# A fourth pair of PSUM banks for the small steps between input and output projection

## The chip, the cores and the metric

The kernel runs on one core of a Trainium2 chip. The metric is the device time of one execution in microseconds (us). A core has a matrix engine (TensorE, in profiles PE), a vector engine (VectorE, DVE), a scalar engine (ScalarE, ACT), a general engine (GpSimd, POOL) and a queue engine that only issues transfers here (SyncE, SP). TensorE writes its results to PSUM, which has eight banks of 128 partitions x 512 float32 values; VectorE and ScalarE read them out. The engines run their own instruction lists in order and meet at semaphores.

## The reference, cut to what matters

One inference step of a two-layer encoder, for a prompt of 256 rows (two tiles of 128, called tile 0 and 1) and a sample of 32 rows (tile 2), all float32:

```
for l in range(2):
    z = rms_norm(x, ln_attn[l]) @ w_in[l]                # input projection, 1024 -> 1184
    # group A: 8 heads, 2 kv heads, QK-norm, rotary, window of 128 rows, learned sinks
    # group B: q from a 256-wide latent (b_w_uq), k and v from a 128-wide latent (b_w_ukv),
    #          norm of every head, shared rotary key, chunk-causal mask, 8 heads
    o = concat(softmax(q_a k_a) v_a, softmax(q_b k_b) v_b)
    x = x + o @ w_o[l]                                   # output projection
    h = rms_norm(x, ln_ffn[l])
    x = x + (swiglu(h) if l == 0 else top2_of_8_experts(h))
```

The new keys, values and latents of both layers are outputs too.

## The kernel before

Each engine's attention work is written out by hand as a list of steps for each layer: `PE_ORDER`, `ACT_ORDER`, `DVE_ORDER`. A step has a kind and a tile, an item or a group:

- `h t`: transpose the normalised rows of tile t (L1645). `za t c q`: input projection of tile t, column half c, reduction half q (L1726); `za 2` (L1696) and `zc t` (L1739) are the rest of it. ScalarE reads `za` out of PSUM by squares and a copy (L908, L909).
- `tq t`: transposes of queries, keys and latents of tile t (L1761 to L1765), after VectorE has normalised and rotated them (`z2`, last instruction L1231).
- `item i`: projection from a latent to keys and values (L1789) or to queries (L1781). VectorE normalises it straight out of PSUM (`i2`: L1375 for keys, L1367 and L1368 for queries, then more steps to L1231), and only then is its PSUM free. `titem i`: its transposes (L1801), copied out by ScalarE (L977).
- `s g`: scores of group g (L1822, L1826, L1836). VectorE adds the mask and takes the maximum (L1400, L1402); ScalarE takes exponentials (L994). For tile 2 the scores stay in PSUM until ScalarE has read them.
- `p g`: transposes of the probabilities (L1851, L1855, L1856), copied out by ScalarE (L1009, L1013). `o g`: probabilities times values (L1883, L1891). `to t`: transposes of the head outputs. `wo t c q` and `wo 2`: output projection (L1726, L1713). `hf t`, `ro t`: what the second half of the layer needs.

`za` and `wo` of tiles 0 and 1 accumulate in bank 0 (column half 0) or bank 1 (column half 1). All other steps are "small" steps and take a pair of banks, a room. There are three rooms, banks 2-3, 4-5 and 6-7, taken in turn over both layers:

```
return small_full, small_out, n % 3, n // 3 + 1, 2 + 2 * (n % 3), 2
```

`wait_room` lets TensorE write a room only after its last tenant was read out (`emptied[i] >= n - 1`); `full` and `free` count fills and releases. So a small step waits until the small step three places earlier in `PE_ORDER` has been read out.

The order of layer 0's small steps around the change: ..., p 0, titem 1, o 0, tq 0, zc 1, titem 2, item 3, s 1, item 4, p 1, tq 1, o 1, titem 3, titem 4, to 2, item 5, wo 2, item 6, s 2, titem 5, s 3, titem 6, hf 2, p 2, s 4, o 2, p 3, ..., s 6, to 0, p 5, s 7, and then the first `wo` of tile 0. In layer 1: ..., titem 2, (last `za` of tile 1), item 4, titem 3, s 1, s 2, o 0, titem 4, p 1, s 3, zc 1, o 1, p 2, to 2, p 3, o 2, o 3, wo 2, tq 1, to 0, ...

After the attention, layer 0 has the dense SwiGLU (L1943, L1959) and layer 1 eight experts in turn (L2027, L2047), whose weights ScalarE and VectorE split into a high and a low part. SP loads all weights through a ring of six slots; a slot is loaded again when the steps that read it are over.

Of the kernel before, what the change touches and what calls it, by code (L numbers as in the profile page):

```python
# [44 lines left out]
DEPTH = 2  # L45
# [105 lines left out]
def in_small(step):  # L151

    return step[0] in OPENS or step in (("za", 2), ("wo", 2))
# [57 lines left out]
    return ev  # L211


def ffn_jobs():

    jobs = [(m, i) for i in range(DCH) for m in ("gate", "up")]
    for c in range(2):
        jobs += [("dn", c, h) for h in range(2)]
        jobs += [("tz", d) for d in range(4 * c, 4 * c + 4)]
    return jobs + [None, ("pos",)]  # L220


def build(nc, a, out, consts):
# [3 lines left out]
    fills = [0] * RING  # L227
# [7 lines left out]
    for n, key in enumerate(plan):  # L235
        prev = [k for k in plan[n % RING:n:RING] if k is not None]
        if key is not None and prev:
# [4 lines left out]
    MOE_EVENTS = moe_events()  # L242
    per_expert = len(EXPERT) // RING
    assert len(EXPERT) % RING == 0
    SMALL = [(s_[0], l, *s_[1:]) for l in range(DEPTH) for s_ in PE_ORDER[l] if in_small(s_)]
    BANKED = [[(s_[0], l, s_[1], c) for l in range(DEPTH) for s_ in PE_ORDER[l] if s_[0] in IN_BANK and s_[2:] == (c, 0)]
              for c in range(2)]
    FFN_JOBS = ffn_jobs()
    place = {key: ("small", n) for n, key in enumerate(SMALL)}
    place.update({key: ("bank", n) for b in BANKED for n, key in enumerate(b)})  # L250
    place.update({key: ("ffn", n) for n, key in enumerate(FFN_JOBS)})
    SQUARES, ROOTS_X, ROWS_X = nth(ACT_ORDER, "zev", "zcev"), nth(ACT_ORDER, "n1", "n2"), nth(DVE_ORDER, "x1", "x2")
# [5 lines left out]
    with ExitStack() as ctx:  # L258
# [3 lines left out]
        def sem(name):  # L262
            return ctx.enter_context(nc.semaphore(name))
# [152 lines left out]
        loaded_cache = sem("loaded_cache")  # L416
        ukv_ready = sem("ukv_ready")
        w_ready = [sem(f"w_ready{i}") for i in range(RING)]
        small_full = [sem(f"small_full{i}") for i in range(3)]
        small_out = [sem(f"small_out{i}") for i in range(3)]  # L420
        bank_full = [sem(f"bank_full{i}") for i in range(2)]
        bank_out = [sem(f"bank_out{i}") for i in range(2)]
        ffn_full = [sem(f"ffn_full{i}") for i in range(4)]
# [85 lines left out]
        def found(key):  # L509

            family, n = place[key]
            if family == "small":
                return small_full, small_out, n % 3, n // 3 + 1, 2 + 2 * (n % 3), 2
            if family == "bank":
                return bank_full, bank_out, key[3], n + 1, key[3], 1
            return ffn_full, ffn_out, n % 4, n // 4 + 1, 2 * (n % 4), 2

        def pair(key, rows=P):

            *_, b, n = found(key)  # L520
            return ps[0:rows, b:b + n, :].rearrange("p a b -> p (a b)")
# [10 lines left out]
        def wait_full(eng, key):  # L532
            filled, _, i, n, *_ = found(key)
            eng.wait_ge(filled[i], n)

        def wait_out(eng, key):
            _, emptied, i, n, *_ = found(key)
            eng.wait_ge(emptied[i], n)

        def wait_room(eng, key):  # L540
            _, emptied, i, n, *_ = found(key)
            if n > 1:
                eng.wait_ge(emptied[i], n - 1)

        def full(ins, key):
            filled, _, i, *_ = found(key)
            ins.then_inc(filled[i], 1)
# [1075 lines left out]
        def _(pe):  # L1623
# [16 lines left out]
            def turn(key, src, rows):  # L1640

                wait_room(pe, key)
                v = pair(key)
                for k in range(KD):
                    ins = tr(v[:, k * P:k * P + rows], src[0:rows, k * P:(k + 1) * P], ident[0:rows, 0:rows])  # L1645
                full(ins, key)

            def turn_back(key, src_T, src):

                wait_room(pe, key)  # L1650
                wait_out(pe, src)
                v = pair(key)
                for t in range(3):
                    ins = tr(v[0:ROWS[t], t * P:(t + 1) * P], src_T[:, TOFF[t]:TOFF[t] + ROWS[t]], ident)
                full(ins, key)

            for l in range(DEPTH):
                for step in PE_ORDER[l]:
                    kind, *which = step
                    if kind == "hf" and l == 1:  # L1660

                        t, = which
                        key, r = ("hf", l, t), ROWS[t]
                        wait_room(pe, key)
                        if t == 1:
                            wait_out(pe, ("wo", l, t, 0))
# [524 lines left out]
```

## Time and profile before

| | us |
|---|---|
| median of 3 runs | 1339.23 (1337.82 to 1339.36) |
| the profiled execution | 1339.84 |
| its span, first to last instruction | 1338.0 |
| attention of layer 0 | about 15 to 176 |
| attention of layer 1 | about 398 to 557 |
| experts | about 557 to 1338 |

The mean granted clock of TensorE over the span is 0.972 of full speed; the granted clock of a stretch (PEclk) is 1.00 at 2.4 GHz and 0.50 at 1.2 GHz. In a row of the timeline the number after the start is the time that the merged instructions took, and the bracket behind it is the idle time of the engine before them, with the instruction that ended it. Rows of transposes show as PE MATMUL with `cst` (the identity) on one side. Times within the span are counted from its start.

### The profile page before, as it was taken

The numbers are of one execution on the slowest core, as the hardware profiler recorded it, in microseconds if no ns is written. First come the engines' busy times: TensorE is split into PE (matmuls) and PEld (weight loads), VectorE is DVE, ScalarE is ACT, GpSimd is POOL, SyncE is SP. The second block draws the span as 40 slices with busy tenths as digits, with TensorE's granted clock in tenths as the row PEclk, the third lists the DMA queues.
The fourth block names the chain that finished last, engine by engine and source line by source line (L and its number), as shares of the span: only waits on it lengthen the run. The fifth ranks groups of instructions, "written<-read, shape, count | busy, mean of one in ns | idle before, by whom it ended". The sixth has DMA issues, their size and how long they took to land.

```text
span 1338.0 us, 18390 instructions
## 1 busy us (share of the span) xinstructions
PE 1285.5 (96%) x6905; PEld 1050.8 (79%) x6905; DVE 938.1 (70%) x917; ACT 795.7 (59%) x793; POOL 146.2 (11%) x130
## 2 busy tenths in 40 slices
PE   5978989999989999999999999999999999999998
PEld 3457579999985467588888888888888888888886
DVE  1647344454334656468898898898898888888987
ACT  2446433433323456256787787777877867867774
POOL 2011000000000010010040040120130300300500
PEclk9978989999999989889999999999999999999999
DMA  8251085544250341669999999999999999999994
GB/s 303 55 122 33 0 253 166 178 158 143 79 185 0 74 125 57 221 237 335 371 383 378 367 396 374 369 397 366 362 411 355 376 397 352 393 387 373 373 405 163
DMA packets 124673, 350.35 MB, mean 262 GB/s; under 512 B 8768, under 2 KB 34080, under 8 KB 124624
## 3 DMA queue, kind: packets, MB, share of 16 engines
q1 hardware_dynamic: 120192, 336.05, 69.0%
q0 software_dynamic: 4032, 12.43, 3.1%
q10 hardware_dynamic: 400, 1.20, 0.2%
q8 instruction: 33, 0.54, 0.2%
q14 instruction: 16, 0.13, 0.0%
HBM read 340.70 MB, written 8.95 MB: 261 GB/s over the span
## 4 chain that ended last, share of the span: by engine, by line
PE 93%; DVE 3%; ACT 2%; issue 1%; DMA 1%; SPq 0%; DVEq 0%; ACTq 0%
PE ps L2027 36%; PE ps L2047 17%; PE ps L1943 11%; PE ps L1726 8%; PE ps L1959 5%; PE ps L1836 1%; PE ps L2035 1%; PE ps L1883 1%; PE ps L1789 1%; PE ps L2001 1%; PE ps L1781 1%; PE ps L1801 1%; PE ps L1645 1%; PE ps L1713 1%; PE ps L1891 1%
## 5 line engine op out<-in xcount | busy, mean ns | idle before, releaser
L1169 DVE TENSOR_TENSOR w_lo<-ring,w_hi 128x2048 fp32r<-128x2048 f32 (+1 forms) x322 | 675.6, 2125 | 180.3 <-ACT w_hi L845 176.8
L845 ACT ACTIVATE w_hi<-ring 128x2048 fp32r<-128x2048 f32 (+1 forms) x322 | 567.3, 1782 | 220.3 <-PE ps L2047 66.4
L2027 PE MATMUL ps<-w_hi,xg_hi 128*128 128x512 f32 (+1 forms) x768 | 288.9, 376 | 0.4 <-DVE xg_lo L1556 0.4
L2027 PE MATMUL ps<-w_hi,xg_lo 128*128 128x512 f32 (+1 forms) x768 | 287.1, 374 | 0.0
L2027 PE MATMUL ps<-w_lo,xg_hi 128*128 128x512 f32 (+1 forms) x768 | 286.2, 373 | 0.0
L2027 PEld LDWEIGHTS ps<-w_hi,xg_hi 128*128 128x128 f32 x768 | 145.2, 189 | 26.3 <-issue 0.5
L2027 PEld LDWEIGHTS ps<-w_lo,xg_hi 128*128 128x128 f32 x768 | 144.9, 189 | 26.0
L2027 PEld LDWEIGHTS ps<-w_hi,xg_lo 128*128 128x128 f32 x768 | 145.2, 189 | 25.2
L2047 PE MATMUL ps<-w_hi,am_hi 128*128 128x512 f32 x340 | 133.8, 393 | 0.0
L2047 PE MATMUL ps<-w_lo,am_hi 128*128 128x512 f32 x340 | 132.5, 390 | 0.0
L2047 PE MATMUL ps<-w_hi,am_lo 128*128 128x512 f32 x340 | 132.4, 389 | 0.0
L1726 PE MATMUL ps<-ring,hT 128*128 128x512 f32 x256 | 114.4, 596 | 0.0
L1943 PE MATMUL ps<-hT_hi,w_hi 128*128 128x288 f32 x352 | 105.3, 299 | 4.1 <-DVE hT_lo L1461 4.1
L789 POOL TENSOR_TENSOR tick<-cst 128x1 f32<-128x1 f32 x22 | 44.9, 2040 | 573.0 <-ACT y_out L1119 473.1
L1943 PE MATMUL ps<-hT_lo,w_hi 128*128 128x288 f32 x352 | 104.8, 298 | 0.0
L1943 PE MATMUL ps<-hT_hi,w_lo 128*128 128x288 f32 x352 | 104.4, 297 | 0.0
L1726 PEld LDWEIGHTS ps<-ring,hT 128*128 128x128 f32 x256 | 47.3, 191 | 52.4 <-issue 52.2
L2047 PEld LDWEIGHTS ps<-w_lo,am_hi 128*128 128x128 f32 x340 | 63.8, 188 | 13.5
L2047 PEld LDWEIGHTS ps<-w_hi,am_lo 128*128 128x128 f32 x340 | 63.9, 188 | 12.9
L2047 PEld LDWEIGHTS ps<-w_hi,am_hi 128*128 128x128 f32 x340 | 63.9, 188 | 12.8
L1943 PEld LDWEIGHTS ps<-hT_hi,w_hi 128*128 128x128 f32 x352 | 66.9, 190 | 4.5 <-issue 4.5
L1943 PEld LDWEIGHTS ps<-hT_hi,w_lo 128*128 128x128 f32 x352 | 67.3, 191 | 0.0
(308 smaller groups left out, 1446.3 us busy)
## 6 DMA issues: line engine op xcount, KB each, us to landing
ring<-in_moe_w_down SPq DMA_DIRECT2D x80, 1024.0 KB, 8.1
ring<-in_moe_w_gate SPq DMA_DIRECT2D x64, 1024.0 KB, 7.2
ring<-in_moe_w_up SPq DMA_DIRECT2D x64, 1024.0 KB, 9.2
ring<-in_moe_w_gate SPq DMA_DIRECT2D x32, 768.0 KB, 7.3
ring<-in_moe_w_up SPq DMA_DIRECT2D x32, 768.0 KB, 6.1
ring<-in_ffn_w_gate SPq DMA_DIRECT2D x11, 1024.0 KB, 5.4
ring<-in_ffn_w_up SPq DMA_DIRECT2D x11, 1024.0 KB, 5.3
ring<-in_ffn_w_down SPq DMA_DIRECT2D x10, 1024.0 KB, 5.1
```

The costliest lines, as they stand in the source:

```text
L789: pool.tensor_tensor(tick[:, i:i + 1], C("ident")[:, 0:1], C("ident")[:, 0:1], ALU.mult)
L845: A(hi[:, 0:size], src[:, 0:size], ACT.Copy).then_inc(hi_ready, 1)
L1169: V.tensor_tensor(lo[:, 0:size], src[:, 0:size], hi[:, 0:size].bitcast(F32), ALU.subtract).then_inc(lo_ready, 1)
L1645: ins = tr(v[:, k * P:k * P + rows], src[0:rows, k * P:(k + 1) * P], ident[0:rows, 0:rows])
L1713: ins = mm_(pair(key)[DEC * j:DEC * j + DEC, 0:256], hT[:, k, TOFF[2]:TOK], slot(wk, 4, 512)[:, k % 4, 256 * (j % 2):256 * (j % 2) + 256], ...
L1726: ins = mm_(pair(key), hT[:, k, TOFF[t]:TOFF[t] + P], slot(wk, 4, 512)[:, k % 4, :], start=(k == 0), stop=(k == KD - 1))
L1781: ins = mm_(pair(key, r)[:, c0:c0 + w], cqT[:, k, TOFF[t]:TOFF[t] + r], slot(("uq", l), 2, 768)[:, k, c0:c0 + w], start=(k == 0), stop=(k ...
L1789: ins = mm_(pair(key, r)[:, c0:c0 + 512], ckvT[:, KOFF[t]:KOFF[t] + r], w_ukv[:, c0:c0 + 512], start=True, stop=True)
L1943: ins = mm_(pair(key)[:, 512 * f:512 * f + TOK], w[:, k, f * P:(f + 1) * P], x[:, k, :], start=(k == 0 and m == 0), stop=(k == KD - 1 and ...
L1959: ins = mm_(pair(("dn", i, d // 2))[:, 512 * (d % 2):512 * (d % 2) + TOK], w[:, k, d * P:(d + 1) * P], x[:, kk, :], start=(kk == 0 and m = ...
L2027: ins = mm_(ps[:, b + c0 // 512, 0:c1 - c0], (xg_hi, xg_lo)[xp][:, k, :], w[wp][:, k % 2, c0:c1], start=(k == 0 and n == 0), stop=(k == KD ...
L2047: ins = mm_(ps[:, 6 + half, :], (am_hi, am_lo)[xp][:, c % 2, k0 + k, :], w[wp][:, k, 512 * half:512 * half + 512], start=(first and k == 0 ...
```

## The change

Between the last `za` of tile 1 and the first `wo` of tile 0, banks 0 and 1 hold nothing. The change makes them a fourth room (number 3) for the small steps of that stretch. `rooms()` gives every small step its room and its number among the fills of the room: inside the stretch the rooms go round by four, outside it by three. The stretch is given by two steps of `PE_ORDER` of each layer, both left out of it: from `za 1 1 1` to `s 7` in layer 0, from `za 1 0 1` to `to 0` in layer 1. Room 3 is taken eight times in layer 0 (tq 0, s 1, o 1, item 5, titem 5, p 2, s 5, s 6) and four times in layer 1 (s 1, p 1, p 2, o 3). The first tenant of room 3 in a layer (tq 0 in layer 0, s 1 in layer 1) also waits until both banks of `za 1` have been read out, and each of the two `wo` of tile 0 waits until all tenants of room 3 have been.

```diff
--- before.py
+++ after.py
@@ -211,6 +211,29 @@
     return ev
 
 
+SPARE_ROOM = [(("za", 1, 1, 1), ("s", 7)), (("za", 1, 0, 1), ("to", 0))]
+
+
+def rooms():
+
+    small, place, fills, last = [], {}, [0] * 4, -1
+    opens, closes = {}, []
+    for l in range(DEPTH):
+        first, end = (PE_ORDER[l].index(step) for step in SPARE_ROOM[l])
+        for i, step in enumerate(PE_ORDER[l]):
+            if not in_small(step):
+                continue
+            last = (last + 1) % (4 if first < i < end else 3)
+            fills[last] += 1
+            key = (step[0], l, *step[1:])
+            small.append(key)
+            place[key] = ("small", (last, fills[last]))
+            if last == 3 and l not in opens:
+                opens[l] = key
+        closes.append(fills[3])
+    return small, place, opens, closes
+
+
 def ffn_jobs():
 
     jobs = [(m, i) for i in range(DCH) for m in ("gate", "up")]
@@ -242,11 +265,10 @@
     MOE_EVENTS = moe_events()
     per_expert = len(EXPERT) // RING
     assert len(EXPERT) % RING == 0
-    SMALL = [(s_[0], l, *s_[1:]) for l in range(DEPTH) for s_ in PE_ORDER[l] if in_small(s_)]
+    SMALL, place, opens_spare, spare_fills = rooms()
     BANKED = [[(s_[0], l, s_[1], c) for l in range(DEPTH) for s_ in PE_ORDER[l] if s_[0] in IN_BANK and s_[2:] == (c, 0)]
               for c in range(2)]
     FFN_JOBS = ffn_jobs()
-    place = {key: ("small", n) for n, key in enumerate(SMALL)}
     place.update({key: ("bank", n) for b in BANKED for n, key in enumerate(b)})
     place.update({key: ("ffn", n) for n, key in enumerate(FFN_JOBS)})
     SQUARES, ROOTS_X, ROWS_X = nth(ACT_ORDER, "zev", "zcev"), nth(ACT_ORDER, "n1", "n2"), nth(DVE_ORDER, "x1", "x2")
@@ -416,8 +438,8 @@
         loaded_cache = sem("loaded_cache")
         ukv_ready = sem("ukv_ready")
         w_ready = [sem(f"w_ready{i}") for i in range(RING)]
-        small_full = [sem(f"small_full{i}") for i in range(3)]
-        small_out = [sem(f"small_out{i}") for i in range(3)]
+        small_full = [sem(f"small_full{i}") for i in range(4)]
+        small_out = [sem(f"small_out{i}") for i in range(4)]
         bank_full = [sem(f"bank_full{i}") for i in range(2)]
         bank_out = [sem(f"bank_out{i}") for i in range(2)]
         ffn_full = [sem(f"ffn_full{i}") for i in range(4)]
@@ -510,7 +532,8 @@
 
             family, n = place[key]
             if family == "small":
-                return small_full, small_out, n % 3, n // 3 + 1, 2 + 2 * (n % 3), 2
+                room, fill = n
+                return small_full, small_out, room, fill, (2 + 2 * room) % 8, 2
             if family == "bank":
                 return bank_full, bank_out, key[3], n + 1, key[3], 1
             return ffn_full, ffn_out, n % 4, n // 4 + 1, 2 * (n % 4), 2
@@ -541,6 +564,11 @@
             _, emptied, i, n, *_ = found(key)
             if n > 1:
                 eng.wait_ge(emptied[i], n - 1)
+            if key in opens_spare.values():
+                for c in range(2):
+                    wait_out(eng, ("za", key[1], 1, c))
+            if key[0] == "wo" and key[2] == 0:
+                eng.wait_ge(small_out[3], spare_fills[key[1]])
 
         def full(ins, key):
             filled, _, i, *_ = found(key)
```

## Rows read from the trace of the kernel before

**Rows 1.** Section 1 of the page: busy time, share of the span and instructions of each engine.

```profile
PE 1285.5 (96%) x6905; PEld 1050.8 (79%) x6905; DVE 938.1 (70%) x917; ACT 795.7 (59%) x793; POOL 146.2 (11%) x130
```

**Rows 2.** Windows, all engines: busy us (x instructions), then PEclk, DMA share, GB/s.

```profile
500.00:1338.00 838.00, 828.71 (x3989) 687.02 (x3987) 700.14 (x477) 594.21 (x424) 119.00 (x62) 0.99 0.91 344
```

**Rows 3.** Waits of PE over the span: us in total, times, longest.

```profile
PE ps L1836 <- DVE rt L1368: 7.0, 2, 4.4
```

**Rows 4.** Timeline, PE, layer 0: start us, us, instructions [idle before <-releaser].

```profile
67.05 0.66 PE L1761 MATMUL ps<-cst,qa 128*128 128x128 f32 x4
...
73.33 2.85 PE L1781 MATMUL ps<-ring,cqT 128*128 128x512 f32 x8
81.03 0.45 PE L1855 MATMUL ps<-cst,sp__65 128*128 128x128 f32 x1 [4.85 <-DVE tmp L1375]
...
81.92 1.06 PE L1761 MATMUL ps<-cst,qa 128*128 128x128 f32 x4
...
86.76 5.64 PE L1891 MATMUL ps<-vb,pT 128*32 128x64 f32 x32 [2.93 <-DVE rt L1368]
92.32 3.52 PE L1801 MATMUL ps<-cst,qkb 128*96 128x128 f32 x16
...
101.30 2.85 PE L1781 MATMUL ps<-ring,cqT 128*128 128x512 f32 x8
...
110.66 3.76 PE L1836 MATMUL ps<-kTb,qTb 96*128 96x128 f32 x16 [4.41 <-DVE rt L1368]
114.21 1.92 PE L1801 MATMUL ps<-cst,qkb 128*96 128x128 f32 x8
...
121.95 1.09 PE L1851 MATMUL ps<-cst,sp__65 128*128 128x128 f32 x8 [0.34 <-ACT sp__65 L994]
...
134.77 3.60 PE L1726 MATMUL ps<-ring,hT 128*128 128x512 f32 x8
```

**Rows 5.** Timeline, DVE (VectorE), layer 0.

```profile
79.86 0.19 DVE L1231 TENSOR_TENSOR kr<-rt,rt 128x32 f32<-128x32 f32 x1
...
112.02 0.42 DVE L1231 TENSOR_TENSOR qkb<-tmp 128x256 f32<-128x256 f32 x1
...
131.50 1.23 DVE L1400 TENSOR_TENSOR sp__65<-ps,cst 128x1024 f32<-128x1024 f32 x1 [1.29 <-PE ps L1836]
```

**Rows 6.** Timeline, ACT (ScalarE), layer 0.

```profile
65.71 0.59 ACT L909 ACTIVATE z<-ps 128x512 f32<-128x512 f32 x1
...
76.02 0.20 ACT L994 ACTIVATION_READ_ACCUMULATOR sp__65<-ps,nb 128x1 f32 x1
...
82.16 0.38 ACT L1013 ACTIVATE pT<-ps 128x256 f32<-128x256 f32 x1 [3.57 <-PE ps L1856]
```

**Rows 7.** Windows of 4 us, layer 0, same columns as rows 2.

```profile
76.00:80.00 4.00, 0.18 (x1) 0.00 (x0) 3.86 (x15) 2.56 (x6) 0.00 (x0) 0.81 1.08 225
...
92.00:96.00 4.00, 4.00 (x22) 3.67 (x22) 0.29 (x1) 1.08 (x2) 0.00 (x0) 0.55 0.00 0
...
108.00:112.00 4.00, 1.34 (x6) 1.37 (x7) 3.84 (x11) 3.53 (x15) 0.00 (x0) 0.65 0.24 82
```

**Rows 8.** Timeline, PE, layer 1.

```profile
458.83 0.75 PE L1826 MATMUL ps<-kTb,qTb 96*32 96x160 f32 x16
462.15 1.16 PE L1836 MATMUL ps<-kTa,qTa 64*128 64x128 f32 x16 [2.57 <-DVE rt L1368]
...
468.09 2.02 PE L1836 MATMUL ps<-kTb,qTb 96*128 96x128 f32 x16 [0.32 <-ACT qTb L977]
...
483.39 5.96 PE L1713 MATMUL ps<-ring,hT 128*32 128x256 f32 x64
```

**Rows 9.** Timeline, ACT, layer 1.

```profile
455.98 0.59 ACT L909 ACTIVATE z<-ps 128x512 f32<-128x512 f32 x1
```

**Rows 10.** Windows, layer 1, same columns as rows 2.

```profile
464.00:468.00 4.00, 3.78 (x17) 2.94 (x16) 3.23 (x8) 1.02 (x2) 0.00 (x0) 0.57 1.07 222
...
479.00:480.00 1.00, 1.00 (x12) 1.00 (x10) 0.97 (x2) 0.78 (x2) 0.00 (x0) 1.00 0.26 102
```

## The prediction

> **What bounds the kernel now.** I read four views in this order. The page and the stretches come first: TensorE is busy 96% of the span, and from 500 us on 828.71 of 838 us at an upper-level clock, while VectorE and ScalarE are filled less [rows 1, 2]. Whatever is won ahead of 500 us therefore reaches the end unless something other than TensorE starts an expert; the expert phase has no term in the sum. The waits of TensorE come second. In the two attention stages the ones to notice are releases by VectorE of PSUM that the next step does not read: L1368 and L1375 read an `item` out of PSUM, but the waiting instructions are L1836 (`s`), L1855 (`p`) and L1891 (`o`), which have nothing to do with an item [rows 3, 4]. They wait for a room. Third, the timeline gives the lengths: 4.85, 2.93 and 4.41 us in layer 0, 2.57 us in layer 1, together 14.8 us [rows 4, 8]. Fourth, the windows give the clock. In layer 0 the level fell to 1.2 GHz at about 78.5 us (mean 0.81 over 76 to 80), some 2.3 us after TensorE ran empty, and rose at about 95.6 us (0.55 over 92 to 96); it fell again at about 109.2 us (0.65 over 108 to 112) [rows 7]. So the waits also make later matmuls slow.
>
> **Why no room wait can get longer.** TensorE works in order. Before, step i needs the room of step i-3; inside the stretch it now needs that of i-4, which step i-1 had to have before. The first few steps of the stretch keep their i-3, and the first tenant of room 3 finds it empty. Everything else of a step's conditions is as it was, and outside the stretch the distance is again 3. So the rotation alone only removes constraints. What is added is two waits where room 3 is opened and one ahead of each of the two `wo` steps of tile 0; they are a few semaphore instructions, costed at nothing if satisfied.
>
> - Opening, layer 0: `tq 0` started at 67.05; the last bank of `za 1` was read by 66.30 (65.71 + 0.59) [rows 4, 6]. Cover 0.75 us, and neither end moves, since nothing ahead of them changes.
> - Opening, layer 1: `s 1` at 458.83 against 456.57 [rows 8, 9]. Cover 2.3 us. If either cover were gone, `tq 0` or `s 1` and all behind it would start later by what is missing.
> - Closing, layer 0: the last tenant of room 3 is `s 6`, read by 132.73; the first `wo` of tile 0 started at 134.77 [rows 4, 5]. Cover 2.0 us, and three other steps of TensorE lie between `s 6` and `wo` whatever moves. Layer 1 closes with `o 3`, long before its `wo`.
> - No DMA, no VectorE and no ScalarE instruction is added or moved. SP's queue waits for the same steps' ends.
>
> **Part A, layer 0, around items 3 and 4.** `item 4` ends at 76.18 (73.33 + 2.85). `p 1` waited for item 3's room; now it has another and needs only the exponentials, ready at 76.22. It starts at 76.4 instead of 81.03 and takes 0.5 us. But what is behind it, `tq 1`, needs VectorE's rows, which end at 80.05 (79.86 + 0.19) [rows 4 to 6]. So most of the first wait turns into a wait for data: `tq 1` starts at 80.1 instead of 81.92, 1.8 us earlier. `o 1` waited for item 4's room until 86.76; now it needs the copy of `p 1`, for which ScalarE had stood idle 3.57 us [rows 6], so it follows `tq 1` directly. TensorE still has 3.2 us without work after `p 1`, so I take the clock to fall as before: `tq 1` at the lower level 1.9 us, to 82.0; `o 1` 5.64 us, to 87.6 instead of 92.3. That is 4.7 us. The block behind it (92.32 to 104.15: two `titem`, `to 2`, `item 5`, `wo 2`, `item 6`) ran 3.3 us at the lower level; starting at 87.6, with the rise some 3.5 us earlier than 95.6, it runs 4.4 us there. Half of the 1.1 us more is lost: 0.5. A = 4.2 us. Bounds: if the level rises only at 95.6, 8.0 us are low, and half of 4.7 us is lost: 2.3. If it never falls, `o 1` takes about 2.8 and ends at 83.8, and VectorE's steps on item 4 (L1368 ended just ahead of 86.76, and `titem 4` needs the steps behind it) become the bound: an estimate of 8.
>
> **Part B, layer 0, around item 6.** `s 3` waited 4.41 us for item 6's room; its new room was `wo 2`'s, read long before. It now runs ahead of the wait. The wait then stands at `titem 6`, which needs VectorE's last step on item 6, done at 112.44: start 112.5 instead of 114.21, 1.7 us earlier [rows 4, 5] (times of before; all of it lies 4.2 us earlier by A). TensorE's idle time is 4.4 us as before, so the clock falls again, and `p 2`, which ran at the upper level, now falls into the lower one. Eight such transposes took 1.92 us at the lower and 1.09 us at the upper level [rows 4], so that costs 0.7 to 0.8 us more. `p 2`'s copy and then the exponentials of group 3 let `p 3` go, which waited 0.34 us at 121.95 [rows 4]. B = 1.0 us; bounds 0 (level low for longer) and 2.8 (level never low). From `p 3` to the end of the output projection TensorE has no such wait, so A + B = 5.2 us reach the dense stage.
>
> **Part C, layer 1.** `s 2` no longer waits 2.57 us; `o 0` does, because its room is now item 4's: it goes at 462.15 instead of about 463.25, 1.1 us earlier [rows 8]. `titem 4` behind it ran at the lower level (0.57 over 464 to 468) [rows 10]; `s 3` waited for its copy until 468.09. If the level stays up, `titem 4`, eight transposes again, is 0.8 to 0.9 us shorter: 2.0 us. If it is low at that place again, 0 to 1. I take 1.5. The output weights have landed by 479.3 (DMA share 0.26 in 479 to 480), and `wo 2` starts at 483.39, so they don't take it back [rows 8, 10].
>
> **Sum.** 4.2 + 1.0 + 1.5 = 6.7 us. The profiled execution took 1339.84 us with a span of 1338.0; it becomes 1333.1 with 1331.3. The median of the runs is 0.6 us lower: 1339.23 - 6.7 = **1332.5 us**.
>
> **Page and trace.** The Trainium skill, TensorE: Matmul & The Clock Gate, under HAM oscillation, reports that PSUM double-buffering added to an already reordered kernel gave nothing further (126.6 to 125.5 us there); by it the result here would be 1339.2, the second rival. The same page, under psum-queue depth-cycling, says that cycling through PSUM banks lets TensorE idle briefly between groups so often that its clock swings; that is the third rival. That the trace's waits end on a room and not on data speaks against the first, for the parts worked out above.
>
> **The rivals.**
> - *The clock stays up.* `p 1` and `s 3` now break up the idle time, and part of the 24 us that layer 0 spent low is given back: A 8, B 2.8, C 2.0, together 12.8 us, 1326.4. For it: every low stretch in these rows follows a wait. Against: the idle pieces left are 3.2 and 4.4 us, and the first fall came 2.3 us after TensorE ran empty. Chance 0.20.
> - *Data takes the room's place everywhere.* `tq 1`, `titem 4` and `titem 6` wait for VectorE, whose chain is barely shorter; if VectorE also sets the pace of `o 1` and of what follows `p 2`, under 2.7 us is left: about 1338. For it: two of four waits do turn into data waits. Against: VectorE was itself idle while TensorE ran `o 1` to `item 5` (0.29 us busy in 92 to 96) [rows 7]. Chance 0.13.
> - *Slower by the clock.* TensorE's idle time comes in more and shorter pieces, and the lower level lasts longer. Its place is layer 0 from 78.5 us and layer 1 from 464 us. Each us more there costs 0.5 us: beyond 13.4 us more than in the bill above the 6.7 us are gone, beyond 18.8 us it is slower by 0.2%; 20 us more give 1342.5. Against: the added steps in the gaps are work, not idleness. Chance 0.04.
> - *As forecast.* Chance 0.63, with its own range 1329 to 1336.
>
> **How the numbers follow.** A change of 2.7 us (0.2%) is about what the measurement can tell from none. The low bounds add up to 2.3 us (1336.9), the high ones to 12.8 (1326.4). The range goes from 1326.5 to 1337.5; it leaves out the faster half of the first rival, part of the second and the third. Faster: 0.63 + 0.20 and a little of the second, less the likeliest case's own tail near no change: 0.84. Same: 0.12. Slower: 0.04.
>
> **What the profile of after would show.** The L1368 wait ahead of L1836 and L1891 and the L1375 wait ahead of L1855 gone in layer 0; instead TensorE waiting about 3 us at L1761 and 4 us at L1801 for L1231 and its neighbours; `o 1` at about 82; `item 6` over at about 100; the dense stage 5 us earlier; in layer 1 a wait of about 1.5 us ahead of L1891 instead of 2.57 ahead of L1836. No wait by ScalarE's L909 at `tq 0`. Wrong would be: the lower level from 78.5 to beyond 96, a wait at the first `wo`, or a gain of layer 0 that is missing at the start of the experts.

## The result, and the profile after

| | before | changed |
|---|---|---|
| median, 8 runs each | 1339.24 | 1341.27 |
| lowest to highest | 1337.82 to 1339.77 | 1340.25 to 1345.64 |
| the profiled execution | 1339.84 | 1340.76 |
| its span, mean granted clock | 1338.0, 0.972 | 1338.9, 0.967 |

The ratio is 1.0025, with a 95% interval of 1.0014 to 1.0036: slower by a quarter per cent, where 0.5% faster was forecast. The time also spreads more, over 5.4 us instead of 2.0. The profiled execution is one of the shorter ones, so the readings below explain less than the whole median. Of two kernels further down, three executions were slow ones of 2156.55, 3508.89 and 5591.87 us, which are left out of every median and ratio here.

The page first. TensorE is busier than before although its instructions are the same ones [rows 1]: 7.2 us more for the same 6905 matmul records.

```profile
PE 1292.7 (97%) x6905; PEld 1058.3 (79%) x6905; DVE 937.8 (70%) x917; ACT 795.8 (59%) x793; POOL 136.4 (10%) x130
```

The waits of TensorE (lines are 28 higher than before: L1829 is `titem`, L1789 `tq`, L1919 `o`, L1864 `s`, L1854 `s 1`, L1809 `item` for queries, L1741 `wo 2`, L1883 `p` of tile 2, L1879 the other `p`, L1754 `za` and `wo`):

```profile
PE ps L1829 <- DVE qkb L1259: 4.8, 2, 4.5
...
PE ps L1789 <- DVE tmp L1403: 4.1, 1, 4.1
PE ps L1919 <- DVE rt L1396: 1.5, 1, 1.5
```

The long waits for L1368 ahead of `s` are gone [rows 3]. In their place stand 4.5 us ahead of `titem 6` and 4.1 us ahead of `tq 1`. The second one is still a wait for a room: `tq 1` stands four places behind item 3 and takes item 3's room. VectorE's timeline shows the rows that `tq 1` transposes done at 79.88 us and the read that frees the room (L1403, L1375 before) only at 80.72:

```profile
79.69 0.19 DVE L1259 TENSOR_TENSOR kr<-rt,rt 128x32 f32<-128x32 f32 x1
...
80.03 0.69 DVE L1403 TENSOR_TENSOR tmp<-ps,rsi 128x512 f32<-128x512 f32 x1
```

The timeline of TensorE in layer 0:

```profile
66.88 0.66 PE L1789 MATMUL ps<-cst,qa 128*128 128x128 f32 x4
...
76.10 0.33 PE L1883 MATMUL ps<-cst,sp__65 128*128 128x128 f32 x1
...
80.87 1.09 PE L1789 MATMUL ps<-cst,qa 128*128 128x128 f32 x4 [4.11 <-DVE tmp L1403]
...
82.74 5.67 PE L1919 MATMUL ps<-vb,pT 128*32 128x64 f32 x32
88.33 3.65 PE L1829 MATMUL ps<-cst,qkb 128*96 128x128 f32 x16
...
97.73 2.85 PE L1809 MATMUL ps<-ring,cqT 128*128 128x512 f32 x8
...
102.51 1.95 PE L1864 MATMUL ps<-kTb,qTb 96*128 96x128 f32 x16
108.92 1.94 PE L1829 MATMUL ps<-cst,qkb 128*96 128x128 f32 x8 [4.46 <-DVE qkb L1259]
...
111.79 1.97 PE L1879 MATMUL ps<-cst,sp__65 128*128 128x128 f32 x8
...
120.86 1.92 PE L1879 MATMUL ps<-cst,sp__65 128*128 128x128 f32 x8
...
126.42 1.97 PE L1879 MATMUL ps<-cst,sp__65 128*128 128x128 f32 x8
...
137.82 2.74 PE L1754 MATMUL ps<-ring,hT 128*128 128x512 f32 x6
```

Set against [rows 4]: `p 1` starts at 76.10 instead of 81.03, `o 1` at 82.74 instead of 86.76, `item 6` at 97.73 instead of 101.30. That is 3.6 us won. `s 3` no longer waits, and `titem 6` does, from 104.46 on. It starts at 108.92 instead of 114.21, 5.3 us earlier. After that the gain melts without a single wait of TensorE: at `p 3` (120.86 instead of 121.95) 1.1 us are left, and the first `wo` of tile 0 starts at 137.82 instead of 134.77, 3.1 us late. Every step in between takes about twice as long as it needs at the upper level: `p 3` 1.92 us for eight transposes instead of 1.09. The windows of 4 us (same columns as [rows 2]) say why:

```profile
76.00:80.00 4.00, 0.67 (x5) 0.36 (x4) 3.86 (x15) 2.89 (x7) 0.00 (x0) 0.85 1.07 222
...
92.00:96.00 4.00, 4.00 (x42) 2.08 (x45) 0.76 (x2) 2.68 (x5) 0.00 (x0) 0.94 0.00 0
...
104.00:108.00 4.00, 0.46 (x5) 0.27 (x3) 3.83 (x10) 3.53 (x13) 0.00 (x0) 0.76 0.35 121
...
112.00:116.00 4.00, 4.00 (x14) 3.21 (x14) 0.59 (x3) 2.21 (x8) 1.95 (x8) 0.50 0.00 0
...
120.00:124.00 4.00, 4.00 (x17) 3.48 (x17) 1.43 (x7) 3.20 (x10) 0.00 (x0) 0.50 0.01 2
...
128.00:132.00 4.00, 4.00 (x29) 4.00 (x28) 2.43 (x9) 3.20 (x10) 0.00 (x0) 0.75 0.00 0
```

Before, the lower level lasted from about 78.5 to 95.6 us and from 109.2 to 116.1 us. Now it lasts from 78.8 to 92.4 and from 106.1 to 130.0 us (ends worked out from the mean clock of windows of 1 us, as in the forecast). The first stretch has become 3.5 us shorter, the second 17 us longer. Counted over the first 600 us, after which the level is up, the lower level holds for 75.1 us before and 88.7 us after (added up from windows of 1 us).

In layer 1 (TensorE's timeline) the loss of layer 0 is carried along and partly made up:

```profile
462.19 0.75 PE L1854 MATMUL ps<-kTb,qTb 96*32 96x160 f32 x16
...
465.51 0.41 PE L1919 MATMUL ps<-cache_v,pT 128*128 128x64 f32 x2 [1.48 <-DVE rt L1396]
...
469.94 3.75 PE L1864 MATMUL ps<-kTb,qTb 96*128 96x128 f32 x16 [0.30 <-ACT qTb L1005]
...
486.33 3.66 PE L1741 MATMUL ps<-ring,hT 128*32 128x256 f32 x64
```

The wait ahead of `o 0` is 1.48 us instead of 2.57 ahead of `s 2` [rows 8], as worked out. `s 1` is 3.4 us late, `s 3` 1.9 us, `wo 2` 2.9 us, the first expert's matmul 1.6 us (575.8 instead of 574.2).

### The profile page after: what moved, and what is told of

The parts are those of the page before. It is cut to its first block, busy times and chain, and to the rows that moved or that the text cites. A ratio compares the mean times of both kernels' runs of the same rounds, so it can differ in the third digit from the quotient of the medians.

```text
span 1338.9 us, 18391 instructions
## 1 busy us (share of the span) xinstructions
PE 1292.7 (97%) x6905; PEld 1058.3 (79%) x6905; DVE 937.8 (70%) x917; ACT 795.8 (59%) x793; POOL 136.4 (10%) x130
## 4 chain that ended last, share of the span: by engine, by line
PE 94%; DVE 3%; ACT 2%; issue 1%; DMA 1%; SPq 0%; DVEq 0%; ACTq 0%
PE ps L2055 36%; PE ps L2075 17%; PE ps L1971 11%; PE ps L1754 8%; PE ps L1987 5%; PE ps L1864 2%; PE ps L1911 2%; PE ps L2063 1%; PE ps L1817 1%; PE ps L2029 1%; PE ps L1829 1%; PE ps L1809 1%; PE ps L1673 1%; PE ps L1879 1%; PE ps L1767 1%; PE ps L2132 1%
## 5 line engine op out<-in xcount | busy, mean ns | idle before, releaser
L1754 PE MATMUL ps<-ring,hT 128*128 128x512 f32 x256 | 114.8, 598 | 0.0
L1971 PE MATMUL ps<-hT_hi,w_lo 128*128 128x288 f32 x352 | 104.7, 297 | 0.0
L817 POOL TENSOR_TENSOR tick<-cst 128x1 f32<-128x1 f32 x22 | 35.8, 1626 | 577.7 <-ACT y_out L1147 470.4
L1754 PEld LDWEIGHTS ps<-ring,hT 128*128 128x128 f32 x256 | 47.5, 191 | 52.7 <-issue 52.5
```

The costliest lines, as they stand in the source:

```text
L817: pool.tensor_tensor(tick[:, i:i + 1], C("ident")[:, 0:1], C("ident")[:, 0:1], ALU.mult)
L1754: ins = mm_(pair(key), hT[:, k, TOFF[t]:TOFF[t] + P], slot(wk, 4, 512)[:, k % 4, :], start=(k == 0), stop=(k == KD - 1))
L1971: ins = mm_(pair(key)[:, 512 * f:512 * f + TOK], w[:, k, f * P:(f + 1) * P], x[:, k, :], start=(k == 0 and m == 0), stop=(k == KD - 1 and ...
```

## The experiments

The theory after this profile: the fourth room does what it says, and the clock takes it back. With `s 3` gone from behind the wait, what follows the idle time is only small work, and the level, once fallen, stays low through it. The rivals: the loss is layer 1's; the room itself costs something; the early part brings the late one into its trouble; the level is of no consequence. Each ratio is to the kernel before, run on the same chip in the same rounds, with its 95% interval; the median of the kernel before lay between 1339.16 and 1339.29 us each time.

**Layer by layer.** Fourth room in layer 0 only, and in layer 1 only. The layer without it keeps three rooms (its stretch is empty and its `wo` has no added wait); the first room of layer 1 is set so that its tail has the rooms of the full kernel:

```diff
-SPARE_ROOM = [(("za", 1, 1, 1), ("s", 7)), (("za", 1, 0, 1), ("to", 0))]
+SPARE_ROOM = [(("za", 1, 1, 1), ("s", 7)), (("to", 1), ("to", 1))]         # layer 0 only
+SPARE_ROOM = [(("to", 1), ("to", 1)), (("za", 1, 0, 1), ("to", 0))]        # layer 1 only
```

> Fourth room in layer 0 only. Theory (the clock): the loss is made in layer 0, where TensorE's level stays at 1.2 GHz from about 106 to 130 us; so this kernel is 2 to 5 us slower than before and has that stretch. Rival (layer 1 or its start is to blame): this kernel is within 1 us of before or 4 us faster, as forecast.

> Fourth room in layer 1 only. Theory (the clock in layer 0 is the whole loss): layer 1 is worth what the forecast said or a little less, 0 to 2 us faster than before. Rival: slower than before by 1 to 3 us.

Layer 0 only: 1341.20 us, ratio 1.0028 (1.0011 to 1.0045). Layer 1 only, eleven runs: 1336.08 us, ratio 0.9982 (0.9964 to 0.9999). The loss is layer 0's. The expectation for layer 0 had its place right and its end wrong: in the profiled execution (1346.09 us, one of the long ones) the second low stretch goes from 107.0 to 141.1 us, 34 us. Its layer 0 has the same instructions as the change, where that stretch lasted 24 us, so the steps alone don't set its length. Layer 1 is faster, but by how much is less clear: its runs and those of the kernel before fall into two groups each (1335.3 to 1336.1 and 1338.7 to 1339.0 us; before, 1335.9 to 1338.1 and 1338.7 to 1340.4, and one of 1350.12). Group against group layer 1 alone is about 0.8 us faster; the rest of the difference is that more of its runs lie in the faster group.

**Half of layer 0.** The stretch of layer 0 ends ahead of item 6, or begins behind `wo 2`; layer 1 as in the change, its first room set as above.

```diff
-SPARE_ROOM = [(("za", 1, 1, 1), ("s", 7)), (("za", 1, 0, 1), ("to", 0))]
+SPARE_ROOM = [(("za", 1, 1, 1), ("item", 6)), (("za", 1, 0, 1), ("to", 0))]   # part A
+SPARE_ROOM = [(("wo", 2), ("s", 7)), (("za", 1, 0, 1), ("to", 0))]            # part B
```

> The stretch of layer 0 ends ahead of item 6, so that s 3 again waits for item 6's room and stands behind the idle time; layer 1 as in the change. Theory (the clock): the low stretch around item 6 is short again, about 7 us, and the 3.6 us won ahead of it reach the end: 3 to 6 us faster than before. Rival (the low stretch comes from the earlier part): as slow as the change, 1 to 3 us slower than before.

> The stretch of layer 0 begins behind wo 2: the waits around items 3 and 4 are as before, only s 3 and what follows has the fourth room; layer 1 as in the change. Theory (the clock): no 3.6 us are won, and the level stays low for some 20 us from 109 us on: 3 to 8 us slower than before. Rival: within 1 us of before.

Part B without A: 1347.62 us, ratio 1.0056 (1.0039 to 1.0072), as expected. Ten of its eleven runs took 1344.45 us or more; of the kernel before, run beside these and the later kernels, two of 79 did. Its windows show the level low from 112.6 to 143.3 us, with TensorE 89% busy in the first row and all of the time after it:

```profile
112.00:116.00 4.00, 3.57 (x20) 3.11 (x21) 3.90 (x7) 1.57 (x5) 3.20 (x10) 0.58 0.00 0
...
120.00:124.00 4.00, 4.00 (x17) 3.35 (x17) 3.00 (x7) 1.41 (x9) 0.00 (x0) 0.50 0.00 0
...
136.00:140.00 4.00, 4.00 (x16) 3.71 (x16) 0.60 (x2) 0.00 (x0) 0.00 (x0) 0.50 0.02 4
```

Part A without B gave no clean answer: ratio 1.0007 (0.9982 to 1.0033), and a median of 1334.86 us that says little, because its ten runs, all of one program, fall into two groups, six from 1331.84 to 1334.92 us with a mean clock of 0.973 to 0.976, and four from 1345.58 to 1345.96 us with 0.967. The profile is of the first group. In it `s 3` waits for its room as before and the low stretch is short, 104.7 to 111.6 us:

```profile
104.00:108.00 4.00, 1.72 (x8) 1.75 (x9) 3.83 (x13) 3.53 (x17) 0.00 (x0) 0.59 0.12 39
108.00:112.00 4.00, 4.00 (x24) 3.60 (x23) 2.75 (x5) 0.42 (x3) 3.51 (x12) 0.56 0.00 0
112.00:116.00 4.00, 4.00 (x29) 3.29 (x28) 1.74 (x4) 3.45 (x11) 1.14 (x6) 1.00 0.00 0
```

and the first `wo` of tile 0 starts 4.4 us earlier than before (130.37 against 134.77); the first low stretch is shorter too, 10.2 us:

```profile
106.28 3.75 PE L1866 MATMUL ps<-kTb,qTb 96*128 96x128 f32 x16 [4.41 <-DVE rt L1398]
...
130.37 3.60 PE L1756 MATMUL ps<-ring,hT 128*128 128x512 f32 x8
```

So both theories of this run are half right: with `s 3` behind the wait the level can come back soon, but in four of ten runs the time is nearly as long as with part B alone. No long run of it was profiled, so where those 12 us went is known only by the mean clock.

**Taking the clock away.** Matmuls that compute nothing are put where TensorE waits. They multiply a constant by 512 columns and write into a room that is free and will be overwritten:

```diff
+            def filler(key, n):
+                wait_room(pe, key)
+                for _ in range(n):
+                    mm_(pair(key)[:, 0:512], ident, w_ukv[:, 0:512], start=True, stop=True)
...
+                    if (l, step) in FILL:
+                        filler(*FILL[l, step])
```

with `FILL` of the full change, its second entry alone, its first alone, and of the kernel before:

```
{(0, ("tq", 1)): (("o", 0, 1), 4), (0, ("titem", 6)): (("hf", 0, 2), 4)}      # change, both gaps
{(0, ("p", 1)): (("tq", 0, 1), 5), (0, ("s", 3)): (("titem", 0, 6), 3)}       # before
```

> The change as it is, with four matmuls of 128x512 (0.9 us each) that compute nothing ahead of tq 1 and four ahead of titem 6 of layer 0, where TensorE has about 4 us without work. Theory (the clock decides what the freed room is worth): the level stays at 2.4 GHz from 76 us to the end of the attention of layer 0, the dense stage starts 8 to 11 us earlier than before, and the time is 8 to 12 us below before with little spread. Rival (VectorE's chain takes the place of the room): the level stays up but the dense stage starts at most 3 us earlier.

> The change with the four matmuls ahead of titem 6 only. Theory: the low level from 106 to 130 us is gone, that from 79 to 92 us stays; 4 to 7 us faster than before. Rival: the low level comes anyway and the time is that of the change, 2 us slower than before.

> The change with the four matmuls ahead of tq 1 only. Theory: the low level from 79 to 92 us is gone, the one behind titem 6 stays and may last from 7 to 24 us or more: between 5 us faster and 3 us slower than before, with a wide spread. Rival (the fourth room is worth its full sum in every case): 8 us faster or more in all runs.

> The kernel before, with five such matmuls ahead of p 1 and three ahead of s 3 of layer 0. It has three rooms, so what it gains is the clock's part alone. Theory: the low stretches of 17 and 7 us go or shrink, 4 to 10 us faster than before; the fourth room then adds some 2 to 5 us in the kernel with both. Rival (the low level costs nothing that counts): within 1 us of before.

| | median | ratio |
|---|---|---|
| change, both gaps filled | 1326.57 | 0.9908 (0.9894 to 0.9922) |
| change, only ahead of `titem 6` | 1330.45 | 0.9936 (0.9923 to 0.9949) |
| change, only ahead of `tq 1` | 1338.58 | 0.9994 (0.9980 to 1.0009) |
| before, two gaps filled | 1335.01 | 0.9966 (0.9948 to 0.9984) |

Eight empty matmuls turn 0.25% slower into 0.9% faster, and the four runs lie within 2.3 us. The timeline of TensorE with both gaps filled (each of these matmuls counts as two in a row, so four are x8; L1691 is the filling, the other lines are 10 higher than in the change):

```profile
76.79 3.60 PE L1691 MATMUL ps<-yT,cst 128*128 128x512 f32 x8
81.06 0.63 PE L1799 MATMUL ps<-cst,qa 128*128 128x128 f32 x4 [0.68 <-DVE tmp L1405]
...
82.06 3.70 PE L1929 MATMUL ps<-vb,pT 128*32 128x64 f32 x32
...
101.33 3.60 PE L1691 MATMUL ps<-yT,cst 128*128 128x512 f32 x8
105.96 1.08 PE L1839 MATMUL ps<-cst,qkb 128*96 128x128 f32 x8 [1.03 <-DVE qkb L1261]
...
125.62 3.60 PE L1764 MATMUL ps<-ring,hT 128*128 128x512 f32 x8
...
170.65 0.58 PE L1981 MATMUL ps<-hT_hi,w_hi 128*128 128x288 f32 x1 [4.15 <-DVE hT_lo L1491]
```

The matmuls from 76.79 and 101.33 us are the filling. `tq 1` starts no earlier than without it; 0.68 us of wait are left. But `o 1` now takes 3.70 us instead of 5.64 or 5.67, the first `wo` of tile 0 starts 9.2 us earlier than before, and the dense stage begins at 170.65, 8.8 us earlier than before (179.4). Of the low stretches in the attention of layer 0 one is left, from 85.7 to 89.1 us. The gap ahead of `titem 6` matters most: filled alone, the low stretch behind it is gone and the time is 8.7 us below before. With only the other one filled the runs spread from 1331.16 to 1342.02 us, and in the profiled one, a short one, the level is low from 105.5 to 119.2 us. The kernel before gains 4.2 us by the two fillings; in its profile the stretch that began at 78.5 us begins at 84.9, and the one at 109 us is gone.

**Dense work inside the low stretch.** In the change, four of these matmuls ahead of `s 4`:

```diff
+FILL = {(0, ("s", 4)): (("s", 0, 4), 4)}
```

> The change, with four 128x512 matmuls that compute nothing ahead of s 4 of layer 0, that is inside the stretch where the level stayed low although TensorE had no gap; they cost 3.6 us at the upper level, 7.2 us at the lower. Theory (the small transposes, scores and value products between 109 and 130 us don't bring the level back up, dense work does): the level rises at about 120 us instead of 130, and the time is 2 us below to 3 us above the change. Rival (the level comes back after a fixed time): it stays low to 130 us and the time is 5 us or more above the change.

1336.76 us, ratio 0.9984 (0.9975 to 0.9993). More work in the place where TensorE already has no gap makes the kernel faster, 4.5 us below the change by the medians. TensorE's timeline and windows:

```profile
108.12 1.94 PE L1839 MATMUL ps<-cst,qkb 128*96 128x128 f32 x8 [4.46 <-DVE qkb L1261]
...
112.73 5.12 PE L1691 MATMUL ps<-yT,cst 128*128 128x512 f32 x8
117.78 1.99 PE L1874 MATMUL ps<-kTa,qTa 64*128 64x256 f32 x8
```

```profile
112.00:116.00 4.00, 4.00 (x10) 2.11 (x9) 0.00 (x0) 3.02 (x12) 1.12 (x6) 0.53 0.00 0
116.00:120.00 4.00, 4.00 (x16) 2.26 (x14) 0.19 (x1) 1.07 (x6) 0.00 (x0) 1.00 0.00 0
```

The level rises at 115.8 us, 3.1 us after the filling began, and stays up through the same small steps behind it that ran low in the change.

**What the fourth room is worth by itself.** The kernel before with all three gaps of layer 0 filled; then both kernels with gaps filled in other places too: ahead of `hf 1` and the dense stage in layer 0, of `h 0` and the routing steps in layer 1, and the gap ahead of `s 2` or `o 0`. In both, TensorE also got a few waits ahead of the fillings at the dense stage and in the routing.

```
before, 3 gaps:   p 1 (5), o 1 (3), s 3 (3)
change, all:      tq 1 (4), titem 6 (4), hf 1 (2), dense (4) | h 0 (3), o 0 (1), routing (1, 1, 2)
before, all:      p 1 (5), o 1 (3), s 3 (3), hf 1 (2), dense (4) | h 0 (3), s 2 (2), routing (1, 1, 2)
```

> The kernel before, with the empty matmuls in all three of its waits of layer 0: five ahead of p 1, three ahead of o 1, three ahead of s 3. Theory (clock and rooms are both worth something): most of the low level of layer 0 goes and it is 5 to 9 us faster than before, but stays 3 us or more above the 1326.6 us of the kernel with the fourth room and the same filling. Rival (all of the gain is the clock's, the fourth room is worth nothing): as fast as that kernel, 1326 to 1328 us.

> The change with the filling ahead of tq 1 and titem 6 of layer 0, and the same in other gaps: ahead of hf 1 (two) and of the dense stage (four) in layer 0, h 0 (three), o 0 (one) and the routing steps (four in all) in layer 1. Theory: the low stretches at the start of the dense stage and of layer 1 shrink, each worth up to 3 us: 1320 to 1326 us. Rival (these gaps are too long or the work there too light for it): 1326 to 1329 us.

> The kernel before with the empty matmuls in all the gaps of the kernel that reached 1312.95 us, placed for its three rooms (ahead of p 1, o 1, s 3 and hf 1 and of the dense stage in layer 0; of h 0, s 2 and the routing steps in layer 1). The level should be up nearly throughout, so the distance to the kernel with four rooms is what the fourth room is worth by itself. Theory (A and B at the upper level gave 3 to 5 us in layer 0, layer 1 about 1): 1316 to 1320 us. Rival (the fourth room is worth nothing once the clock is up): 1312 to 1314 us.

Before with three gaps filled: 1333.03 us, ratio 0.9946 (0.9933 to 0.9960), 6.5 us above the change with both gaps filled; its profile still has a low stretch in layer 0, 90.5 to 93.9 us, and one of 10 us in layer 1, so that is not the room's part alone. The change with all gaps filled: 1312.95 us, ratio 0.9815 (0.9800 to 0.9829), 26 us below before, better than either theory had it. Its stretches, to the end of the span:

```profile
70.00:136.00 66.00, 63.76 (x431) 43.83 (x429) 43.38 (x104) 39.59 (x111) 9.96 (x26) 1.00 0.26 67
136.00:340.00 204.00, 202.57 (x1394) 187.46 (x1394) 91.44 (x67) 75.47 (x63) 0.00 (x0) 1.00 0.50 160
340.00:500.00 160.00, 154.77 (x975) 109.97 (x973) 87.21 (x212) 73.99 (x170) 6.42 (x12) 1.00 0.30 86
500.00:1308.00 808.00, 801.24 (x3893) 665.99 (x3892) 686.21 (x450) 580.64 (x391) 113.65 (x60) 1.00 0.94 355
```

The clock is at 1.00 in all of them, 0.999 over the span; the 24 us at the lower level around the first expert are gone too, which the expectation hadn't counted on. Before with all gaps filled: 1320.01 us, ratio 0.9865 (0.9846 to 0.9884), mean clock 0.997 in the profiled execution. The quotient of the two ratios is 0.995: with the level up nearly throughout, the fourth room is worth 6.8 us by them (their intervals leave 3.5 to 10), 7.1 by the medians. The starts of the dense stage and of the first expert, in the change and in the kernel before, all gaps filled, show where:

```profile
168.25 0.37 PE L1991 MATMUL ps<-hT_hi,w_hi 128*128 128x288 f32 x1 [0.68 <-DVE hT_lo L1491]
...
547.49 0.49 PE L2078 MATMUL ps<-w_hi,xg_hi 128*128 128x512 f32 x1 [0.93 <-DVE xg_lo L1586]
```

```profile
172.94 0.37 PE L1963 MATMUL ps<-hT_hi,w_hi 128*128 128x288 f32 x1 [0.68 <-DVE hT_lo L1463]
...
556.95 0.49 PE L2050 MATMUL ps<-w_hi,xg_hi 128*128 128x512 f32 x1 [0.93 <-DVE xg_lo L1558]
```

The dense stage starts 4.7 us apart, of which 0.7 us stood already at `item 4` (73.22 and 73.94), ahead of the waits that the change moves: 4.0 us for layer 0. From there to the first expert 4.8 us more come in. The kernel before spends 6.8 us of that stretch at the lower level (517 to 527 us, in two pieces), worth 3.4 us, so 1.4 us are left for layer 1. Together that is 5.4 us in these two executions. They ran on different chips and have 22 and 26 filling matmuls; in layer 0 of the kernel before, `p 1`, `o 1` and `s 3` still waited 0.2 us each behind their filling, so it delayed none of them.

## Why the prediction was wrong, point by point

- *Rooms only remove constraints, the added waits are covered.* Right. `tq 0` starts at 66.88 with no wait, and none stands at the first `wo`. The waits moved to the places that the text named (`tq 1`, `titem 6`, `o 0`), but at `tq 1` for another reason than it gave.
- *Part A, 4.2 us.* 3.6 us measured at `item 6`. The lower level lasted 13.6 us, to 92.4, as assumed. Two readings in it were off. "Most of the first wait turns into a wait for data": by the text's own i-4, `tq 1` needs item 3's room, so it started at 80.87 and not at 80.1. And `o 1` with the level up took 3.70 us (both gaps filled), not 2.8.
- *Part B, 1.0 us, bounds 0 and 2.8.* This is the step that failed. Its first half was right: `titem 6` started 5.3 us earlier than before where A and B's start gave 5.9. The failing sentence is that the clock "falls again" and costs "0.7 to 0.8 us more". The price assumed that the level would come back about as soon as before. It came back 13.9 us later (130.0 instead of 116.1), and from `titem 6` to the first `wo` 8.4 us were lost (5.3 early, then 3.1 late). With that gap filled the stretch is gone and the kernel is 0.64% faster than before. The low bound of 0 was no bound: nothing in the rows limited how long the level would stay low.
- *From `p 3` on TensorE has no such wait, so the gain reaches the dense stage.* The first half held; the conclusion didn't, because TensorE, without a wait, ran at half its clock up to 130.0 us.
- *Part C, 1.5 us.* 2.4 us by the ratio of layer 1 alone (0.9982, but its interval reaches from nothing to 4.8 us), 3.2 by the medians, about 0.8 group against group, 1.4 in the last two profiles. The wait of 1.48 us stood where it was put.
- *The rival "slower by the clock", chance 0.04.* It is what happened, with its place and its price. The bill had the first stretch of layer 0 as measured, and the second as short as before or 1.5 us longer. So the change had some 16 to 17 us more of the lower level there than the bill. At the rival's 0.5 us each that is about 8 us, 1.3 or so more than the 6.7; measured is 2.0 us slower by the medians, 0.9 in the profiled executions. One part of the rival was not so: TensorE's idle time did not come in more pieces in layer 0. It was given almost no chance because "the added steps in the gaps are work": but `p 1` and `s 3` were taken from behind the gaps. What stood there before, 3.76 us of `s 3` at the lower level, was followed by the rise. That its place is the reason is argued; what the runs show is how often the time is long: with `s 3` ahead of the wait and no part A in ten of eleven runs, in the kernel before in two of 79.
- *The sum of 6.7 us.* That it is close to the worth of the room with the clock held up, 6.8 to 7.1 us, is in part luck: it was added up for a clock that falls, and by the profiles the room gives 4.0 us in layer 0 (5.2 in the sum) and 1.4 in layer 1 (1.5). The first rival's 1326.4 us for a clock that stays up was met by the change with both gaps filled, 1326.57; there 8.8 us were won at the dense stage, where that rival had 10.8.

The filling shows the cause by taking it away, and the filling of `titem 6`'s gap shows the place. Not settled is what sets how long the level stays low. Behind a gap of 4.46 us and the same steps it was 13.7 us with only `tq 1`'s gap filled, 23.9 in the change and 30.7 with part B alone. With part A alone it was 7 us in one execution and, to judge by the time and the mean clock, much more in others; no long run of that kernel was profiled.

On the page that was weighed: the Trainium skill, TensorE: Matmul & The Clock Gate, says under psum-queue depth-cycling that cycling through banks makes the clock swing and costs throughput. This trace agrees that the level is lost around idle time (it fell at 106.1 us, inside the wait of 4.46 us) and that it costs throughput. But most of the cost came without any idle time: the lower level went on for 21 us in which TensorE had none. Its remark under HAM oscillation, that PSUM double-buffering gave nothing further, fits the change as it stands (ratio 1.0025); with the level up the room gave 0.5% here.

## What to carry to other kernels

When a wait goes, ask what the engine does right behind the next one. Here a gap of 4.46 us with small matmuls behind it was followed by 14 to 34 us at half the clock, which cost more than the gap itself, and the change that shortened the waits lengthened that stretch. Price the level as an unknown of its own, with its own high end, and test it by putting a few dense matmuls that compute nothing into the gaps: here the change with all gaps filled gained 1.85% by the ratio (26 us by the medians), where the change alone lost 2 us and the filling without the fourth room gained 1.35%. Then count the rooms for every step behind the change, not only for those that waited before: a wait for a room can move to the next step and look like one for data.

## What the runs showed of the hardware that was not expected

- The lower level outlives the gap by far: in the change, 21 us of work without a gap, from 108.9 to 130.0 us; with part B alone, on to 143.3 us. In the change, four dense matmuls ahead of `s 4` made the difference: with them the level was up 3.1 us after they began.
- One program can have two times. Part A alone ran in 1331.8 to 1334.9 or in 1345.6 to 1346.0 us, nothing between, with mean clocks of 0.973 to 0.976 and 0.967. The kernel before did so too, rarely: 77 of 79 runs took 1335.1 to 1341.0 us, two took 1350.12 and 1351.05, with a mean clock of 0.965.
- The level can be held up for a whole execution, through gaps and small work: a mean of 0.999 over 1308.4 us in the profiled execution, 0.993 to 0.997 in the other four.
